# Hybrid decoder step on one core: queries projected in one visit, squares from turned tokens, tables counted apart, page numbers read once per pair, nine convolutions beside the delta rules

## What is computed

```python
xn = rmsnorm(x, norm1)
q, k, v, qkv_b, z, b_raw, a_raw = project(xn, w_in, q_norm, k_norm)
oa = softmax(q1 k1) v - lam * softmax(q2 k2) v          # differential attention, paged cache for samples
qkv_b = silu(sum(conv_w[j] * xpad[:, j:j + t] for j in range(4)))   # short causal convolution
q, k = l2norm(qb) * DKB ** -0.5, l2norm(kb)
S = exp(G_last) * S + delta^T (exp(G_last - G) * k)     # gated delta rule, chunks of 64 tokens
x = x + concat(rmsnorm(oa), rmsnorm(ob) * silu(z)) @ w_out
x = x + peer_ffn(rmsnorm(x, norm2))                     # 8 heads x 16 of 16384 experts per token
```

## Time and profile before

| what | us |
|---|---|
| median of 3 timed runs | 2055.15 (2053.49 to 2056.07) |
| the profiled execution, its own time | 2046.96 |
| its span | 2045.1 |
| PE busy, whole span | 1691.6 (83%) |
| DVE busy | 1335.3 (65%) |
| first matmul of the output projection (L2151) | 456.18 |

### The profile page before, as it was taken

The page is one execution under the profiler, slowest core; times in us unless marked ns, Lnnn a source line. Parts: engine busy times, 40 slices in busy tenths (PEclk is TensorE's granted clock), DMA queues, the critical chain, the costliest instruction groups (busy, mean ns, idle before and its releaser), DMA issues.

```text
span 2045.1 us, 20559 instructions
## 1 busy us (share of the span) xinstructions
PE 1691.6 (83%) x6211; PEld 853.0 (42%) x6211; DVE 1335.3 (65%) x3023; ACT 802.0 (39%) x2371; POOL 785.1 (38%) x670
## 2 busy tenths in 40 slices
PE   7697999988897878989787888978997657866777
PEld 2242464547453445445344544533563213522111
DVE  1344514344897657897665888775688967679544
ACT  1342322131645523563453346354344423333332
POOL 2111110111444444435444353534444555554442
PEclk9798999999999989999898999999999888987999
DMA  9999823226999999999999999999999999999997
GB/s 333 358 309 382 263 92 118 93 104 244 406 414 409 427 428 428 426 426 411 428 421 429 426 426 400 416 426 393 427 427 426 427 427 427 427 427 427 427 427 313
DMA packets 137015, 758.91 MB, mean 371 GB/s; under 512 B 15263, under 2 KB 24495, under 8 KB 60472
## 3 DMA queue, kind: packets, MB, share of 16 engines
q0 software_dynamic: 88448, 622.22, 73.4%
q1 hardware_dynamic: 44976, 128.07, 16.8%
q10 hardware_dynamic: 3480, 7.31, 1.0%
HBM read 741.56 MB, written 16.26 MB: 371 GB/s over the span
## 4 chain that ended last, share of the span: by engine, by line
PE 38%; DMA 30%; DVE 16%; ACT 7%; issue 4%; SPq 3%; POOL 2%; ACTq 0%; DVEq 0%; POOLq 0%
DMA sb_uv<-in_peer_uv,sb_eidx 27%; PE bank L2224 16%; PE bank L1827 8%; DVE sb_uv L1806 7%; PE bank L2151 3%; PE bank L2191 2%; DVE sb_hres L1780 2%; SPq L841 1%; POOL sb_uv L1006 1%; SPq L845 1%; ACT sb_diag L1384 1%; DMA sb_w<-in_w_sections 1%; PE bank L1941 1%; ACT sb_ew L1377 1%; PE bank L1953 1%
## 5 line engine op out<-in xcount | busy, mean ns | idle before, releaser
L2224 PE MATMUL bank<-sb_uv,sb_diag 128*128 128x512 f32 (+1 forms) x1860 | 943.2, 643 | 277.8 <-ACT sb_diag L1384 267.8
L1006 POOL DMA_INDIRECT sb_uv<-in_peer_uv,sb_eidx x576 | 704.1, 1222 | 829.8 <-PE bank L2224 646.4
L1806 DVE CUSTOM_DVE_ANT_0 sb_uv<-sb_uv,sb_xn 128x1024 f32<-128x1024 f32 x576 | 698.9, 1220 | 280.5 <-DMA sb_uv<-in_peer_uv,sb_eidx 277.6
L2224 PEld LDWEIGHTS bank<-sb_uv,sb_diag 128*128 128x128 f32 (+1 forms) x1860 | 333.8, 194 | 766.4 <-ACT sb_diag L1384 440.7
L1373 ACT ACTIVATE sb_gel<-sb_h 128x1 f32<-128x1 f32 x576 | 116.3, 202 | 753.5 <-DVE sb_h L1806 750.4
L1827 PE MATMUL bank<-sb_w,sb_xnT 128*128 128x512 f32 (+1 forms) x560 | 270.3, 626 | 24.7 <-DMA sb_w<-in_w_sections 11.7
L1384 ACT ACTIVATE sb_diag<-sb_stay,sb_ew 128x128 f32<-128x128 f32 (+1 forms) x465 | 183.2, 394 | 45.7 <-PE bank L2224 2.5
L1377 ACT ACTIVATE sb_ew<-sb_gel,sb_gate 128x1 f32<-128x1 f32 x576 | 169.7, 295 | 19.8
L1827 PEld LDWEIGHTS bank<-sb_w,sb_xnT 128*128 128x128 f32 (+1 forms) x560 | 100.6, 190 | 149.8 <-issue 122.6
L1780 DVE SCALAR_TENSOR_TENSOR sb_hres<-sb_uv,sb_ew,sb_hres 128x1024 f32<-128x1024 f32 x111 | 142.2, 1281 | 0.1
L2191 PEld LDWEIGHTS bank<-sb_rT,sb_zone 128*128 128x128 f32 x832 | 99.3, 193 | 15.7 <-issue 15.3
(11 more groups left out here) (352 smaller groups left out, 1593.2 us busy)
## 6 DMA issues: line engine op xcount, KB each, us to landing
sb_zone<-in_w_route SPq DMA_DIRECT2D x11, 2304.0 KB, 11.8
sb_w<-in_w_sections SPq DMA_DIRECT2D x40, 512.0 KB, 7.3
sb_zone<-in_w_mixer SPq DMA_DIRECT2D x8, 2048.0 KB, 15.6
sb_uv<-in_peer_uv,sb_eidx POOLq DMA_INDIRECT x576, 14.0
sb_sS<-in_cache_kT SPq DMA_DIRECT2D x32, 256.0 KB, 7.3
sb_zone<-in_cache_kT SPq DMA_DIRECT2D x32, 256.0 KB, 7.2
sb_held<-in_cache_v SPq DMA_DIRECT2D x32, 256.0 KB, 7.0
sb_zone<-in_cache_v SPq DMA_DIRECT2D x32, 256.0 KB, 5.9
```

What stands on the lines that cost most here:

```text
L1006: nc.gpsimd.indirect_dma_start(uv[:, m % RING, :], None, i["peer_uv"], bass.IndirectOffsetOnAxis(ap=eidx[:, t % 2, n:n + 1], axis=0)).then ...
L1806: nc.vector.tensor_tensor_reduce(out=uv[:, m % RING, 0:D], in0=uv[:, m % RING, 0:D], in1=xn2[:, t % 2, :], scale=1.0, scalar=0.0, op0=ALU. ...
L2224: ins = nc.tensor.matmul(bank[half][0:rows, :], lhsT=G["diag"][:, d % DIAGS, 0:rows], rhs=uv[:, m % RING, D + 512 * half:D + 512 * half + ...
```

## The change

Six edits, all in the first part:

- q is visited for all five tiles in the third visit, so there are nine visits and 36 pieces instead of ten and 40; units still number 35, and the last visit is now k of tiles 0 to 3. The turned q of tiles 0 to 3 all go to DRAM and are loaded back one tile at a time (`query_load`, now for tile 0 too). The buffer sb_qst is taken by t % 2 with one semaphore for each half.
- x_prompt is no longer loaded. ACT squares the turned tokens before they are scaled, and PE sums over the 1024 features (`square_sums`: eight matmuls of one column against the constant -1/2 into bank 7 per tile). DVE may scale sb_xnT only after that tile was squared. The loads of the turned tokens are all issued at once.
- The tables' semaphore is split: s_early counts w_ba and the early tables, whose loads now stand ahead of the first value pages, and s_stay the stay tables, which are loaded later, and the second norm's gains (issued by SP instead of POOL).
- The value pages of a pair take their page numbers from the registers that the key pages of the same pair filled: 64 of 128 reads go.
- The convolutions get an order of their own, `CONVS`. The first six are those of tiles PT and 0; the other nine are due from early_at(215) on in steps of 17, beside `gdn(0)` and `gdn(1)`, which wait only for what tile PT needs. Convolution buffer 1 moves from sb_hres to sb_resident, and the router weights that live there are loaded when all convolutions are done.
- The due times of the units are laid out anew, and four of the counts in waits follow.

```diff
-VISITS = [(4, [PT]), (5, [PT]), (6, [PT])] + [(g, ORDER) for g in range(4)] + [(g, list(range(PT))) for g in range(4, NSEC)]
+VISITS = [(4, [PT]), (5, [PT]), (6, ORDER)] + [(g, ORDER) for g in range(4)] + [(g, list(range(PT))) for g in (4, 5)]
-C0 = 3
+C0 = 2 + NT
-QK = [("k", PT), ("q", PT)] + [("k", t) for t in range(PT)] + [("q", t) for t in range(PT)]
+QK = [("k", PT), ("q", PT)] + [("q", t) for t in range(PT)] + [("k", t) for t in range(PT)]
+CONVS = [(sec, n) for sec in range(3) for n in range(2)] + [(sec, n) for sec in range(3) for n in range(2, NT)]
...
 def conv_at(m):
-    return after(C0 + m, 13)
+    sec, n = CONVS[m]
+    return after(C0 + NT * sec + n, 13) if n < 2 else early_at(215 + 17 * (m - 6))
...
                     for n, t in enumerate(ORDER):
-                        yield early_at((0, 28.9, 42, 46, 50)[n])
+                        yield early_at((0, 28.9, 29.0, 29.1, 29.2)[n])
...
                 def x_squares(n):
-                    act.wait_ge(s_x[n], 32 if t == PT else 16)
...
+                    nc.scalar.activation(xin[n].rearrange("p (k r) -> p k r", k=KC), xT(t), ACT.Square).then_inc(s_xsq, 1)
...
+                        if n:
+                            dve.wait_ge(s_xsq, n)
                         nc.vector.tensor_tensor(xT(t), xT(t), F["gain1"][:, :].unsqueeze(2).broadcast_to([128, KC, ROWS[t]]), ALU.mult).then_inc(s_xnT, 1)
...
+                def square_sums(n):
+                    yield early_at(SUMMED[n] + 0.3)
...
+                    pe.wait_ge(s_xsq, n)
+                    for k in range(KC):
+                        ins = nc.tensor.matmul(bank[7][:, n:n + 1], lhsT=xin[n][:, 128 * k:128 * k + 128], rhs=minus_half[:, 0:1], start=k == 0, stop=k == KC - 1)
+                    ins.then_inc(s_ss, 1)
...
-                    dve.wait_ge(s_tables, 48)
+                    dve.wait_ge(s_early, 32)
...
                 def value_loads(p):
...
-                            pages = []
-                            for g in range(4):
-                                n = (2 * p + seq) * NPG + 4 * half + g
-                                pages.append(sp.value_load(F["pages"][0:1, n:n + 1], min_val=0, max_val=i["cache_v"].shape[0] - 1))
+                            pages = pages_of[p, half, seq]
...
-                        dve.wait_ge(s_nrm, NT + 1)
-                        dve.wait_ge(s_cs, 2 * NT + 1)
+                        dve.wait_ge(s_nrm, 3)
+                        dve.wait_ge(s_cs, 5)
```

More of the change, by code:

```diff
@@ L369, in hybrid_step @@
         s_ident = sem("identity_and_gain1_loaded")
-        s_tables = sem("tables_loaded")
-        s_x = [sem(f"x_loaded{r}") for r in range(NT)]
+        s_early = sem("gate_columns_and_early_tables_loaded")
+        s_stay = sem("stay_tables_and_gain2_loaded")
+        s_x = sem("sample_rows_loaded")
+        s_xsq = sem("turned_tokens_squared")
         s_gain = sem("qk_gains_loaded")
@@ L393, in hybrid_step @@
         s_kst = [sem(f"k_stored{r}") for r in range(2)]
-        s_qst = sem("q_spilled")
+        s_qst = [sem(f"q_spilled{r}") for r in range(2)]
         s_vst = sem("v_stored")
@@ L495, in conv_loads, with taps_loads, normed_before @@
         def conv_loads(m):
-            return sum((1 if k % NT else 1 + CONV_W) for k in range(m + 1) if conv_buffer[k] == conv_buffer[m])
+            return sum((1 if CONVS[k][1] else 1 + CONV_W) for k in range(m + 1) if conv_buffer[k] == conv_buffer[m])
+        def taps_loads(m):
+            return sum(k == 0 or CONVS[k][0] != CONVS[k - 1][0] for k in range(m + 1))
+        def normed_before(m):
+            return sum(CONVS[k][0] < 2 for k in range(m))
         def conv_before(m):
@@ L507, in spill_count @@
         def spill_count(m):
-            return sum(k % NT > 0 for k in range(m % 3, m + 1, 3))
+            return sum(CONVS[k][1] > 0 for k in range(m % 3, m + 1, 3))
         def kst_count(u):
@@ L517, in hybrid_step @@
             entries.append(("unit", n))
-            if n == C0:
+            if n == 3:
                 entries += [("turn", 0), ("turn", 1)]
-            entries += [("turn", u) for u in range(2, 2 * NT) if n == QK_UNIT[u] + (2 if QK[u][0] == "k" else 1)]
+            entries += [("turn", u) for u in range(2, 2 * NT) if n == QK_UNIT[u] + 1]
         entries.append(("turn", 2 * NT - 1))
@@ L1152, in conv_silu @@
                         act.wait_ge(s_vecs, 112)
-                        if m >= 2:
-                            act.wait_ge(s_bss, m - 1)
-                            act.wait_ge(s_bms, m - 1)
+                        if m < 2:
+                            for spilled in s_qst:
+                                act.wait_ge(spilled, 32)
+                        if j >= 2:
+                            act.wait_ge(s_bss, j - 1)
+                            act.wait_ge(s_bms, j - 1)
                         for h in range(NH):
-                            cols, k = slice(h * HD, (h + 1) * HD), NH * (m % 2) + h
-                            ins = nc.scalar.activation(F["qst"][0:rows, m % 2, cols], dst[:, cols], ACT.Square, accum_out=F["bss"][0:rows, k:k + 1])
+                            cols, k = slice(h * HD, (h + 1) * HD), NH * (j % 2) + h
+                            ins = nc.scalar.activation(F["qst"][0:rows, j % 2, cols], dst[:, cols], ACT.Square, accum_out=F["bss"][0:rows, k:k + 1])
                         ins.then_inc(s_bss, 1)
@@ L2040, in attention_head @@
                     if h == 0 and n == 0:
-                        for kind, k in (("unit", V0), ("turn", 0), ("turn", 2), ("turn", NT + 1)):
+                        for kind, k in (("unit", V0), ("turn", 0), ("turn", NT + 1)):
                             b, at = entry_bank(kind, k)
                             pe.wait_ge(s_bank[b], at + 1)
-                    if h == 0 and n:
-                        pe.wait_ge(s_qt, 16 * n)
+                    if h == 0:
+                        pe.wait_ge(s_qt, 16 * (n + 1))
                     if h == 0 and n + 1 == PT:
@@ L2202, in queries @@
                     ins.then_inc(s_s2p, 1)
-                work = [Stream(unit(n)) for n in range(len(UNITS))] + [Stream(turn(u)) for u in range(2 * NT)] + [Stream(small_columns()), Stream(decay_totals())]
+                work = [Stream(unit(n)) for n in range(len(UNITS))] + [Stream(turn(u)) for u in range(2 * NT)] + [Stream(square_sums(n)) for n in range(1, NT)] + [Stream(small_columns()), Stream(decay_totals())]
                 work += [Stream(gdn(u)) for u in range(NT)] + [Stream(sample_updates(h)) for h in range(NH)]
```

200 lines of the change are left out of this document (105 added, 95 removed).

## The result

The changed kernel took 2065.77 us (median of 8 runs, 2060.72 to 2074.83) against 2052.26 us before (8 runs, 2046.91 to 2056.07): a ratio of 1.0071, interval 1.0052 to 1.009. It is slower by 0.7%, some 14 us. The prediction was 16 us faster; 2065.77 lies outside the range of 2018 to 2057.

What follows compares the result with a forecast made beforehand. Before the gathers, which keep DMA busy from 600 us, SP's list was taken as the limit. Gains of 42 us less 7 gave a 35 us lead; less 19 given back, 16 us faster: 2039 us, range 2018 to 2057.

Steps and rivals of the forecast that it cites:

- term 2: First keys: q units of tile 0 to 3 fill the place where PE waited for keys, gaining 4.1 us.
- rival C: Early part bound by DMA, not SP's list: lead near 20 us, time 2054, no change; chance 0.12.
- D: Shared reads leave SP's queue as late as before: 12.1 us stay lost, gain 4 us, 2051; chance 0.07.
- Rival B: Slower: nine convolutions stop the delta rules' level chain, 4.5 us lost for each, 2061 us; chance 0.11.
- The lead of 35 us: Time gained when the delta rules are reached: 42 us of gains less 7 for square sums.
- term 5: Delta rule's start: its 3.17 us wait behind a convolution on DVE goes as that convolution moves; 3.2 us gained.
- term 7: Square sums: eight one-column matmuls for each of four tiles add 7 us of PE work in the early part.
- the 12.5 and 12.1 us for tables and page numbers: Early waits: 12.5 us before the gate columns, and 12.1 us of late weights and slow clock, both go.
- Term 4: DMA bytes: 4 MB fall away, about 11 us of the DMA engines, with nothing counted on its own.
- The 19 us given back: Delta rules to attention's start: four places lacking unit cover lose 7.9, 3.9, 3.2 and 4.2 us.
- the 3.2: Start of gdn(1) waits behind the next convolution's rows, as gdn(0)'s did: 3.2 us lost.
- The shared read port: DVE multiplications hold up POOL's z products 1.44 us each, 7 us if all five; in the range only.

Runs made afterwards that it cites:

- e1_store_first: The changed kernel with the store of tile PT's new keys issued right after they are normalised, ahead of the first page loads: 2045.75 us, ratio to before 0.9971.
- e3_convs_by_unit: e1_store_first with the convolutions back in the order of their units, only one behind the start of gdn(0): 2046.91 us, ratio to before 0.9976.
- e8_rows_five_earlier: e1_store_first with POOL issuing late convolutions' rows and taps ahead of the samples' power and the previous convolution's z gain: 2028.5 us, ratio to before 0.9892.
- b1: The kernel before with only the shared page numbers (value pages use the key pages' registers): 2051.79 us, ratio 0.9996.
- b3: The kernel before with the shared page numbers and the early tables ahead of the first values on their own semaphore: 2045.5 us, ratio 0.9972.

## Why the prediction was wrong

- **The first units and the store of k** (term 2). The step that failed is "the q units of tile 0 to 3 stand where PE waited. 4.1 us go". The wait for the keys did go, but the step counted the units as free filler and did not ask which buffer they write. sb_qkn was reused in the last visits before and in the next units now, and its release hung on a store in the middle of SP's list, which the order showed (out_k_sample behind eight value loads, in the excerpt). A wait of 22.9 us, worth 20 by e1_store_first, was in no term and no rival. It alone turns the sign. By the prediction's own signs, gdn(0) after 248 us would have meant C or D and an attention after 427 us B; the changed kernel has 265 and 439, and the cause is in none of the three.
- **The lead of 35 us.** Without that wait it was 32 at gdn(0): right in size, but by luck and not by its terms. By e3_convs_by_unit 24 of the 32 come from moving the nine convolutions, for which the sum had 3.2 (term 5), and 8 from all the rest, for which it had 31.8. The square sums of term 7 took what was counted, 1.84 us a tile. Of the 12.5 and 12.1 us for tables and page numbers, the parts alone in the kernel before gave 4 and 0 at the end, both 6. Term 4, "I count nothing for it on its own", left out the bytes; full DMA engines (rival C, given 0.12) are the reading that fits the early part of the kernel before, and the rows of the late convolutions, which left that part, were in no term as bytes.
- **The 4 MB.** HBM read fell from 741.56 to 740.77 MB. The taps are loaded six times instead of three, because the late convolutions return to all three sections; with the old order (e3_convs_by_unit) the page says 737.63. The prediction missed these three loads of 1 MB.
- **The 19 us given back.** It was 26.5 in e1_store_first: 32 us of lead at gdn(0), 5.7 at the mixer. The mechanism, DVE behind a convolution whose rows POOL issued late, was right, and so was the first place: 7.56 us for a forecast of 7.9, though POOL stood there behind the samples' power and not behind z of tile PT. That z stood ahead of the second stop's rows (issued at 284.60), but took 1.26 us; POOL had waited 21.29 us before it for the power of the convolution before. The second stop was 2.95 us, and DVE in it also waited 1.61 us for ACT's squares. In e1_store_first the copies took 2.46 for 3.9, gdn(1) 1.98 for 3.2, the last chunk and the start of attention 1.42 and 4.49 for 4.2. The last three are the same in e8_rows_five_earlier (1.98, 1.42, 4.49), so they do not come from late rows, and the reason given for the 3.2 was wrong. The sample updates, 2.29 us in the changed kernel and 0.59 before, were not in the sum.
- **Rival B** was named with the right sign and the wrong cause. The slower time came from the store. Its own mechanism, convolutions stopping the level chain, is there and took back 26.5 us, not more than the 32; e8_rows_five_earlier brings that down to 8 us (33 us of lead at gdn(0), 25 at the mixer) with the same work on DVE, so most of it was when the rows were asked for. The argument against B that DMA is only 0.27 busy there held for 300 to 350 us; the rows of the first stop landed in a stretch with a share of 1.06.
- **The shared read port.** One of the five z products was hit, 3.02 us at 324.04 beside a multiplication that began on DVE at 323.63; the longest of the others took 1.27. The port also works the other way: at 283.43, beside a z product that POOL had begun at 283.38, a product of DVE (L1491) took 1.76 us, against 0.69 for the same one at 300.44. Both agree with the rule that the prediction draws from the Trainium skill (SBUF — State Buffer, Who interferes with whom). Neither is near the size of the miss; leaving it out of the sum did no harm.

## What to carry to other kernels

When work is moved forward, follow every buffer that it writes to whoever empties it, and look up where that emptying stands in its own engine's list; a store or a load behind someone else's wait costs as much as the wait. When the DMA engines are full, as in b1 and b3, shortening the list that feeds them can change only which transfer is last: take bytes out of the full stretch, and ask for them in a slack one, ahead of anything in that list that waits. Here two steps stuck in such lists, both mended by due times alone, were the difference between a loss of 14 us and a gain of about 23.

## What was not expected

The window from 250 to 300 us has a DMA share of 0.56, and yet a load of 1 MB of rows behind 1 MB of taps took 14.7 us to land in it (260.35 to 275.05), against a median of 8.4 us for the 1 MB rows. The average hides a full stretch: the share was 0.25 from 250 to 260 us and 1.06 at 378 GB/s from 260 to 275. Before a share is taken for room, it has to be read over the transfer's own time.

Two kernels with PE timelines that differ by 24 us at 245 us came out level at 450 (e1_store_first, e3_convs_by_unit), which the times at the end do not show.
